# First stage of a hybrid transformer layer: float32 projections and modulation rows rewritten as split fp32r products and vector sums

## The reference, cut to what matters

```
mod_x = silu(c) @ w_mod + b_mod          # 6 rows of 1024: shift 1, scale 1, gate 1, shift 2, scale 2, gate 2
mod_c = silu(c_ctx) @ w_mod + b_mod
hx = rms_norm(x, norm_mix_g) * (1 + sc1) + sh1       # 1024 latent tokens; hc: 256 context tokens
fx, qx, kx, vx = split_projection(hx @ w_in)         # 256 | 768 | 256 | 256 columns
qx, kx = axial_rope(heads(qx, 12, q_norm_g)), axial_rope(heads(kx, 4, k_norm_g))
kc = heads(kc, 4, k_norm_g)                          # of the context only k and v are used
attn_x = softmax(q k^T / 8) v over 1024 + 256 keys
x = x + g1 * (concat(fourier(fx), attn_x) @ w_out)
x = x + g2 * expert_choice_ffn(modulate(x, norm_ffn_g, sh2, sc2))    # 16 experts, 128 tokens each
out = rms_norm(x, final_norm_g)
```

## Time and profile before

| | |
|---|---|
| median of 3 runs | 2188.39 us (2185.91 to 2189.53) |
| the profiled execution: its time, its span | 2189.9 us, 2188.1 us |
| busy in the span: TensorE, VectorE, ScalarE, GpSimd | 1969.8, 1576.8, 1259.7, 271.7 us |
| first stage | 0 to 361.9 us |
| Fourier block | 361.9 to 393.8 us |
| attention | 393.8 to 1003.9 us |
| experts and final norm | 1003.9 to 2188.1 us |

### The profile page before, as it was taken

One profiled execution on the slowest core, in us unless ns is written; L12 is line 12 of the kernel. 1 busy time (PEld: TensorE's weight loads), 2 busy tenths in 40 slices (PEclk: granted clock), 3 DMA queues, 4 the chain that ended last, 5 costly groups with the idle time before them and its releaser, 6 DMA issues.

```text
span 2188.1 us, 28420 instructions
## 1 busy us (share of the span) xinstructions
PE 1969.8 (90%) x8917; PEld 1486.1 (68%) x8917; DVE 1576.8 (72%) x1985; ACT 1259.7 (58%) x1830; POOL 271.7 (12%) x305
## 2 busy tenths in 40 slices
PE   6899988898899889981699999999999999999993
PEld 2444467566666666651588888888888888888882
DVE  0255541577666766656798999889998899888993
ACT  1222110567665766552477777777767777777762
POOL 0122210011110111010120110101101011010111
PEclk9899999899999999995799999999999999999996
DMA  8411155501110111002799999999999999999985
GB/s 259 155 77 77 58 192 187 129 27 49 58 41 26 48 58 41 26 19 106 269 410 393 384 379 382 390 390 386 381 376 396 384 393 377 379 385 394 379 322 199
DMA packets 107298, 513.31 MB, mean 235 GB/s; under 512 B 12488, under 2 KB 37488, under 8 KB 56944
## 3 DMA queue, kind: packets, MB, share of 16 engines
q1 hardware_dynamic: 99728, 489.34, 58.3%
q0 software_dynamic: 4608, 16.78, 3.0%
q10 hardware_dynamic: 2912, 6.55, 0.8%
HBM read 479.09 MB, written 33.55 MB: 234 GB/s over the span
## 4 chain that ended last, share of the span: by engine, by line
PE 48%; issue 2%; DVE 2%; DMA 1%; POOL 0%; ACT 0%; ACTq 0%; POOLq 0%; SPq 0%
PE banks L1402 31%; PE banks L1427 15%; PE banks L1414 1%; PE banks L1383 1%; DVE topi L1275 1%; DVE top L1273 1%; DVE cand L1276 0%; DMA xe<-h_scratch,idx_g 0%; DMA acc_scratch<-ysc,idx_s 0%; DVE raw L1366 0%; DMA fgain<-in_final_norm_g 0%; ACT raw L1259 0%; DMA raw<-acc_scratch 0%; POOL carry L1153 0%; POOL idx_g L1158 0%
## 5 line engine op out<-in xcount | busy, mean ns | idle before, releaser
L1307 DVE TENSOR_TENSOR w_lo<-raw,w_hi 128x2048 fp32r<-128x2048 f32 x256 | 574.8, 2287 | 67.7 <-ACT w_hi L1208 67.7
L1208 ACT ACTIVATE w_hi<-raw 128x2048 fp32r<-128x2048 f32 x256 | 470.2, 1917 | 7.6 <-DMA raw<-in_w_exp 7.5
L1402 PE MATMUL banks<-w_hi,x_hi 128*128 128x512 f32 x1024 | 405.5, 396 | 1.4 <-DVE x_lo L1301 1.4
L1402 PE MATMUL banks<-w_hi,x_lo 128*128 128x512 f32 x1024 | 400.1, 391 | 0.0
L1402 PE MATMUL banks<-w_lo,x_hi 128*128 128x512 f32 x1024 | 399.5, 390 | 0.0
L1315 DVE TENSOR_TENSOR d_lo<-raw,d_hi 128x1024 fp32r<-128x1024 f32 x256 | 296.2, 1218 | 2.1 <-ACT d_hi L1230 2.0
L1230 ACT ACTIVATE d_hi<-raw 128x1024 fp32r<-128x1024 f32 x256 | 258.0, 1060 | 35.0 <-DMA raw<-in_w_exp 20.0
L1402 PEld LDWEIGHTS banks<-w_hi,x_lo 128*128 128x128 f32 x1024 | 192.8, 188 | 40.8
L1402 PEld LDWEIGHTS banks<-w_hi,x_hi 128*128 128x128 f32 x1024 | 193.0, 188 | 39.7 <-DVE x_lo L1301 1.8
L1402 PEld LDWEIGHTS banks<-w_lo,x_hi 128*128 128x128 f32 x1024 | 193.2, 189 | 38.2
L908 DVE TENSOR_TENSOR ptl<-banks,pth 128x384 fp32r<-128x384 f32 x320 | 176.3, 554 | 56.8 <-ACT pth L854 51.8
(11 more groups left out here) (195 smaller groups left out, 2627.3 us busy)
## 6 DMA issues: line engine op xcount, KB each, us to landing
raw<-in_w_exp SPq DMA_DIRECT2D x384, 1024.0 KB, 7.7
unit<-in_w_mod SPq DMA_DIRECT2D x12, 1024.0 KB, 7.8
q_scratch<-qst SPq DMA_DIRECT2D x8, 1536.0 KB, 5.2
win<-in_w_mod SPq DMA_DIRECT2D x12, 1024.0 KB, 12.4
qt<-q_scratch SPq DMA_DIRECT2D x32, 384.0 KB, 4.2
win<-in_w_in SPq DMA_DIRECT2D x2, 2048.0 KB, 13.5
xt<-in_x SPq DMA_DIRECT2D x8, 512.0 KB, 3.3
xr<-in_x SPq DMA_DIRECT2D x8, 512.0 KB, 4.0
```

Source lines behind the costliest of these rows:

```text
L1208: act.activation(w_hi[which][c][:, :], raw[which][c][:, :], ACT.Copy).then_inc(s["hi_done"], 1)
L1307: dve.tensor_tensor(w_lo[which][c][:, :], raw[which][c][:, :], w_hi[which][c][:, :].bitcast(F32), ALU.subtract).then_inc(s["lo_done"], 1)
L1402: i = pe.matmul(psum[:, 2 * (j % 2) + which, :], x_[par][:, k, :], w_, start=(k == 0 and w_ is hi and x_ is x_hi), stop=(k == KD - 1 and x ...
```

## The change

The first stage becomes a function of its own, `nc_phase_a`, with the loops written out.

- Projections: `w_in` is loaded as three packed blocks of 2 MB and split once into `w_hi` (fp32r) and `w_lo`. The modulated tile is split into `h_hi` and `h_lo`. Each float32 matmul becomes three fp32r ones of 512 columns (72 per latent tile, 24 per context tile).
- Modulation columns: all eight units are loaded at once into eight places; TensorE's matmuls for them are as before.
- Modulation rows: the 16 units go to VectorE, two per latent tile. Each unit comes in two halves through three ring buffers of 512 KB; eight dependent instructions of 256 columns sum it over the contraction's eight blocks into `acc`, TensorE adds the 128 partitions with a column of ones, ScalarE copies the row of 256 back into `acc`, and GpSimd issues a DMA that adds it to `mod_scratch` in DRAM, where `b_mod` was put before. There are two `acc` buffers, so that a unit waits for the store of the unit two before it (`row_out_done`).
- q and k: VectorE no longer splits them before the transposes. TensorE transposes 8 float32 pieces per latent tile; ScalarE rounds them on the way out, VectorE subtracts. SyncE then writes q in two DMAs and k in four per tile.
- Attention: queries are read with two DMAs per group instead of one; the four rows are loaded broadcast from `mod_scratch`, with two GpSimd instructions for scale 2.
- Experts: the first gather uses `icol` directly (no copy, no `carrier`); the wait for `fgain` and its scaling move from before the token choice to behind the last expert loop.
- Tables are packed for longer transfers.

The diff, cut to its core:

```diff
@@ build, before: VectorE's split, TensorE's projection and rows @@
-                        after(dve, s["qkt_done"], (n - TC) * QTG + TC)
-                    if kind == "lat":
-                        vq = hv(v[:, 0:QW]).unsqueeze(2).broadcast_to([P, NQ, 2, HD])
-                        dve.tensor_copy(hlq[:, :, 0, :, :], vq)
-                    chain(dve.tensor_copy(hlk[:, :, 0, :], hv(v[:, QW:QK])))
-                    if kind == "lat":
-                        dve.tensor_tensor(hlq[:, :, 1, :, :], vq, hlq[:, :, 0, :, :].bitcast(F32), ALU.subtract)
-                    dve.tensor_tensor(hlk[:, :, 1, :], hv(v[:, QW:QK]), hlk[:, :, 0, :].bitcast(F32), ALU.subtract).then_inc(s["hl_done"], 1)
...
-                        pe.wait_ge(s["win_kv_in" if n == 0 else "win_in"], 16 if n == 0 else 32)
-                    after(pe, s["prj_done"], n)
-                    for c in ((1, 0, 2) if kind == "lat" else (2,)):
-                        for k in range(KD):
-                            i = pe.matmul(psum[:, PJ + c, :], ht[par][:, k, :], win[:, k, c * 512:(c + 1) * 512],
-                                          start=(k == 0), stop=(k == KD - 1))
-                    i.then_inc(s["proj_done"], 1)
...
-                        pe.wait_ge(s["row_done"], u - 5)
-                    for k in range(KD):
-                        i = pe.matmul(psum[:, ROW_BANKS[u % 6], 0:UM], c_wide[:, k, :], row_unit[u % 8][:, k, :],
-                                      start=(k == 0), stop=(k == KD - 1))
-                    i.then_inc(s["row_mm"], 1)
...
@@ nc_phase_a, SyncE @@
+            for u in range(NC_UNITS):
+                sp.dma_start(slot[u][:, :, :].rearrange("p k n -> p (k n)"), w_mod[u]).then_inc(unit_in[u], 16)
+            for c in (2, 1, 0):
+                sp.dma_start(w_raw[:, c, :, :].rearrange("p k n -> p (k n)"), w_in[c]).then_inc(w_raw_in[c], 16)
+                if c == 2:
...
+            def load(i):
+                if i < RING:
+                    sp.wait_ge(s["unit_used"], NC_UNITS)
+                else:
+                    sp.wait_ge(s["mod_used"], i - RING + 1)
+                half = w_mod[NC_UNITS + i // 2][:, i % 2 * HALF_UNIT:(i % 2 + 1) * HALF_UNIT]
+                sp.dma_start(ring[i % RING][:, :], half).then_inc(ring_in[i % RING], 16)
+            def store(n):
+                sp.wait_ge(s["qlo_done"], qt_count(n + 1))
+                for par in range(2):
+                    rows_ = slice(par * HD, (par + 1) * HD)
+                    if lat(n):
+                        sp.dma_start(q_d[n - TC].rearrange("(j b) d n -> b d j n", b=2)[par],
+                                     qst[rows_, 0:6, :, :].rearrange("p j a n -> p j (a n)").bitcast(F32)).then_inc(s["q_out"], 16)
+                    for h in range(2):
+                        sp.dma_start(ks[h * HD:(h + 1) * HD, par:NKV:2, n * P:(n + 1) * P].bitcast(F32), qst[rows_, 6:8, h, :].bitcast(F32)).then_inc(s["k_out"], 16)
...
@@ nc_phase_a, GpSimd @@
+            def row_out(u):
+                if u == 0:
+                    pool.wait_ge(s["preset"], 16)
+                pool.wait_ge(s["row_ev"], u + 1)
+                pool.dma_start(mod_d[u * UM:(u + 1) * UM].unsqueeze(0), acc[u % 2][0:1, :], accum_op=ALU.add).then_inc(row_out_done[u % 2], 16)
+            rstd(0)
+            for n in range(TS + 1):
+                if n + 1 < TS:
+                    rstd(n + 1)
+                if n >= 1:
+                    squares(n - 1)
+                    rstd16(n - 1)
+                    for u in units_of(n - 1)[1:]:
+                        row_out(u)
+                if n < TS:
+                    for u in units_of(n)[:1]:
+                        row_out(u)
+            for i in range(2):
+                pool.wait_ge(row_out_done[i], 16 * NR_UNITS // 2)
...
@@ nc_phase_a, ScalarE and VectorE @@
+            def high(n):
+                act.wait_ge(s["hf_done"], 2 * n + 2)
+                act.activation(h_hi[n % 2][:, :, :], h_f[n % 2][:, :, :], ACT.Copy).then_inc(s["hh_done"], 1)
+            def weights(c, half):
+                act.wait_ge(w_raw_in[c], 16)
+                if c < 2:
+                    act.wait_ge(s["unit_used"], 2 if c == 1 else 4)
+                k = slice(4 * half, 4 * half + 4)
+                act.activation(w_hi[:, c, k, :], w_raw[:, c, k, :], ACT.Copy).then_inc(s["wh_done"], 1)
...
+            def modulation(u, half):
+                i = 2 * u + half
+                dve.wait_ge(ring_in[i % RING], 16 * (i // RING + 1))
+                if half == 0:
+                    after(dve, row_out_done[u % 2], 16 * (u // 2))
+                else:
+                    dve.wait_ge(s["mod_used"], i)
+                for k in range(4):
+                    w = ring[i % RING][:, k * UM:(k + 1) * UM]
+                    c = c_sig[:, 4 * half + k, 0:1]
+                    if half == 0 and k == 0:
+                        ins = dve.tensor_scalar(acc[u % 2][:, :], w, c, None, ALU.mult)
+                    else:
+                        ins = dve.scalar_tensor_tensor(out=acc[u % 2][:, :], in0=w, scalar=c, in1=acc[u % 2][:, :], op0=ALU.mult, op1=ALU.add)
+                    if k < 3:
+                        link(ins)
+                ins.then_inc(s["mod_used"], 1)
+            dve.wait_ge(s["silu_done"], 1)
...
+            for n in range(TS + 2):
+                if 1 <= n <= TS:
+                    values(n - 1)
+                if n >= 2:
+                    queries(n - 2)
+                if 1 <= n <= TS:
+                    scaled(n - 1)
+                units = units_of(n) if n < TS else ()
+                for u in units[:1]:
+                    modulation(u, 0)
+                    modulation(u, 1)
+                if 1 <= n <= TS:
+                    sums(n - 1)
+                for u in units[1:]:
+                    modulation(u, 0)
+                if 1 <= n <= TS:
+                    rotate(n - 1)
+                for u in units[1:]:
+                    modulation(u, 1)
+                if n < TC:
+                    for half in range(2):
+                        weights(1 - n, half)
...
@@ nc_phase_a, TensorE @@
+            def project(n, c):
+                if c == 2 and not lat(n) or c == 1:
+                    pe.wait_ge(s["hl_done"], n + 1)
+                free, v = {0: ("ev0", n - TC), 1: ("ev1", n - TC), 2: ("v_done", n)}[c]
+                after(pe, s[free], v)
+                if n == (0 if c == 2 else TC):
+                    pe.wait_ge(s["wl_done"], w_parts(c) + 2)
+                    if c == 2:
+                        pe.wait_ge(s["c_row_done"], NC_UNITS)
+                for k in range(KD):
+                    for x_, w_ in ((h_hi, w_hi), (h_hi, w_lo), (h_lo, w_hi)):
+                        i = pe.matmul(psum[:, PJ + c, :], x_[n % 2][:, k, :], w_[:, c, k, :], start=(k == 0 and x_ is h_hi and w_ is w_hi),
+                                      stop=(k == KD - 1 and x_ is h_lo))
+                i.then_inc(s[f"pj{c}"], 1)
...
+                pe.wait_ge(s["mod_used"], 2 * u + 2)
+                if u > 0:
+                    pe.wait_ge(s["row_ev"], u)
+                else:
+                    pe.wait_ge(s["cols_done"], 2)
+                pe.matmul(psum[0:1, MB, 0:UM], ones[:, 0:1], acc[u % 2][:, :], start=True, stop=True).then_inc(s["row_mm"], 1)
+            for u in range(NC_UNITS):
+                if u == 1:
...
+            for n in range(TS):
+                if not lat(n):
+                    project(n, 2)
+                    turn(n + 1, 0)
+                    turn(n + 1, 1)
+                else:
+                    project(n, 1)
+                    for u in units_of(n - 1)[1:]:
+                        row(u)
+                    if n + 1 < TS:
+                        turn(n + 1, 0)
+                    project(n, 0)
+                    if n + 1 < TS:
+                        turn(n + 1, 1)
+                    row(units_of(n)[0])
+                    project(n, 2)
+                if n >= 1:
+                    queries(n - 1)
+            row(NR_UNITS - 1)
+            queries(TS - 1)
+    return unit_in
@@ nc_phase_m, GpSimd, gather @@
+                if isinstance(e, int) and e == 0:
+                    pool.indirect_dma_start(out=xe[:, :], out_offset=None, in_=h2_d,
+                                            in_offset=bass.IndirectOffsetOnAxis(ap=icol[:, 0:1], axis=0)).then_inc(s["x_in"], 16)
+                    return
```

More of the change, by code:

```diff
@@ L122, in build @@
         f_tok = sb("f_tok", [P, TL, FW], F32, K)
+        unit_in = nc_phase_a(nc, sem, a, psum, ident, ones, eps_c, ks, vs, f_tok, q_d, mod_d, x_d, ctx_d, w_mod, w_in)
         y_t = sb("y_t", [P, 2, N], F32, K)
-        A = ExitStack()
-        unit = [sb(f"unit{i}", [P, KD, UM], F32, A) for i in range(2)]
-        win = sb("win", [P, KD, IN], F32, A)
-        vec = sb("vec", [5 * KD, P], F32, A)
-        c_sig = sb("c_sig", [P, KD, 2], F32, A)
-        bg_col = sb("bg_col", [P, 3 * KD], F32, A)
@@ L165, in build @@
```

(29 more changed lines are left out.)

699 lines of the change are left out of this document (343 added, 356 removed).

## The result

| | before | changed |
|---|---|---|
| median | 2188.37 us (2185.91 to 2189.53, 4 runs) | 2111.09 us (2110.05 to 2115.79, 4 runs) |
| profiled execution: its time, its span | 2189.9, 2188.1 us | 2115.79, 2114.0 us |
| first stage ends | 361.9 us | 297.69 us |
| Fourier block takes | 31.85 us | 29.52 us |
| attention takes | 610.09 us | 608.95 us |

The ratio is 0.9652 (95% interval 0.9635 to 0.9669), 3.5% less. The forecast was 2116 in a range of 2076 to 2146. Of the 74.1 us by which the span is shorter, 64.2 lie in the first stage, 5.9 at the experts' start, 2.3 in the Fourier block and 1.7 in the rest.

What follows compares the result with a forecast made beforehand. The prediction took TensorE to bound the first stage before the change, and VectorE's pass with its store wait after. Its sum: 2189.9 − 66.5 (first stage) + 0.5 (attention) − 7.0 (experts) = 2116.9, stated as 2116, range 2076 to 2146 us.

Steps and rivals of the forecast that it cites:

- The wait: First stage, each pass: VectorE's half unit waits for GpSimd's store, issued only behind the power; 7 to 8 us idle.
- L: First stage: time from issue to landing of GpSimd's row store, taken as 4.4 us, range 2.6 to 6.2.
- VectorE's own work in a pass: First stage, per latent tile: a pass takes 20.8 us besides the store's time from issue to landing.
- The period: First stage: one pass per latent tile takes 25.2 us, against 26.75 before.
- TensorE's work: First stage, per latent tile: 19.2 us, 19.6 with hand-overs, hidden under VectorE's pass.
- The head: Start of the first stage: first latent projection at 77 us, before 83.6; bounds 71 and 85.
- The end of the stage: Last latent tile: rotary step over at 286.2, six stores issued in 2.4, first stage over at 295.4 us.
- Experts: Start of the expert stage: 3.4 us at the token choice and 4.5 before the first gather saved; 7.0 kept.
- (A): First stage: the store's wait doesn't bind and TensorE sets the period at 19.6; 2078 us, chance 0.11.
- (B): First stage: the store is slow, like a DMA of 11.8 us; period 32.6, 2168 us, chance 0.12.
- (C): First stage: idle stretches keep TensorE at 1.2 GHz throughout; period 38.4, 2222 us, chance 0.03.
- (D): First stage: something else, ScalarE or SyncE, keeps the period at 26.75; 2127 us, chance within the forecast's 0.74.

Runs made afterwards that it cites:

- e1: Changed kernel with three accumulator buffers instead of two, so the half unit needs a store issued a pass ago: 2080.9 us.
- e2: Changed kernel, still two accumulator buffers, with GpSimd issuing the odd unit's store ahead of the head norm's power: 2088.1 us.
- e6: e1 with the whole second unit under the power and SyncE requesting the fourth half unit ahead of the q and k stores: 2077.1 us.
- e4: Changed kernel with both edits at the expert stage's start undone (early final-gain scaling; copy and carrier before first gather): 2116.9 us.

## Why the prediction was right

It was right in its main step, and the number partly by two errors that cancel. Point by point:

- **The wait.** The order head sums, power, store, half unit is in the trace, and e1 and e2 show that it binds. The place of the wait and what stands behind it are as predicted.
- **L, the time from issue to landing.** Taken as 4.4 us, measured as 2.15 in the pass shown, and over all 16 stores 2.0 (least), 2.1 (median), 5.7 (most). This is the term that was mis-sized: my middle between the earlier trace rows was too near to the scatter with its 512 KB. The Trainium skill (DMA: Bandwidth & Descriptors, "Anatomy of one DMA — SWDGE (gpsimd) path") gives about 2.0 us as the fixed part of the whole time of such a DMA, and the trace agrees; the prediction's 3.0 came from adding the time to the first byte on top.
- **VectorE's own work in a pass.** Predicted 20.8 us beside L, measured 24.74 − 2.15 = 22.6. A dependent instruction of the unit costs 0.52 (seven in 3.67) and not 0.45, which makes 1.0 for 14 of them; GpSimd's squares hold VectorE for another 1.5 here, which the prediction did not have. The rotary part is shorter, 5.0 and not 5.3, and the rest of the 0.7 between these terms and 22.6 lies in small steps. The idle time was to be 7 to 8 us and is 5.4. So L came out 2.2 too long and VectorE's work 1.8 too short, and the pass of 25.2 is near to 24.74 by luck.
- **The period.** 25.2 predicted, 24.74 in the pass shown, 25.65 on average: one pass had a store that landed late (idle 9.1 us), another 6.5.
- **TensorE's work.** 19.2 us, 19.6 with hand-overs. The changed kernel doesn't show it, but e6 does: a period of 19.71 with TensorE busy throughout. The low clock cost 1.6 to 3.0 us in five tiles of the changed kernel, where 2.5 a tile were allowed.
- **The head.** First projection at 50.4 (47.7), first latent projection at 77.10 (77), VectorE's pass behind the first latent projection at 97.7 (98.5). Units and the first tile's transposes were over at 39.7 (37.0): they began at 9.2 instead of 8, and the first unit took 5.2 us instead of 3.5. The second tile made up for it.
- **The end of the stage.** Rotary part over at 286.48 (286.2), stage end at 297.69 (295.4), in an execution 4.7 us above the median. The six stores take 5.6 us to issue and not 2.4:

```profile
285.25 1.23 DVE L484 TENSOR_TENSOR a_qkn<-a_qkn,a_sq 128x1024 f32<-128x1024 f32 x1
...
289.89 0.62 SPq L240 DMA_DIRECT2D q_scratch<-a_qst  x1
...
293.38 2.13 SPq L243 DMA_DIRECT2D ks<-a_qst  x2
...
297.69 0.43 ACTq L676 DMA_DIRECT2D chan<-in_chan  x1
```

- **Experts.** 5.9 saved in the profile, 5.8 by e4; 7.0 predicted out of 7.9. The rows above show the missing 2: the gather is now issued under the two `w_lo` of 4.49 us, its issue takes 2.87 us instead of 1.13, and it lands 8.1 us after its start instead of 6.6. The prediction had bounded this loss at 2 to 4 from the row of the copy, and its sentence with the rule of the Trainium skill (SBUF — State Buffer, "SBUF: two separate sides") made the sum 1.4 worse; the trace agrees with that.
- **Attention.** 0.5 more predicted, 1.1 less measured, which is inside the spread of 606.3 to 609.5 us between kernels with the same attention. The Fourier block's 2.3 us were not predicted, and no run was made on their cause.
- **Rivals.** (A) described e6 and not this kernel; its 2078 is what the kernel takes once both waits are gone (2077.1). (B) shows in one pass only. (C) is wrong: TensorE's clock did fall behind stops, but 3.5 to 6.4 us into a tile's matmuls it was back at full speed (five tiles of the changed kernel). (D) named the danger rightly, a period like before's, and at 25.65 the mean is not far from its 26.75; but it is the forecast's wait that makes it, not another.

## What to carry to other kernels

Before counting what a faster form of the matmuls brings, find what the bound engine will wait for: here the split was worth about 5 us with two accumulators, and 36 us in the kernel with a third one of 1 KB a partition and the unit under the power. A small store that frees a buffer belongs ahead of anything long on its queue, or the buffer should be one deeper. And when work is moved under a wait, its loads must be moved with it.
